# The key-value latent and the rotary key as two column halves of 288 in an encoder block

## The reference

```python
h = rms_norm(x, norm_mix_g[l])
z = h @ w_in[l]                      # columns: 4096 conv | 512 c_q | 512 c_kv | 64 k_pe | 4096 gates
u_conv, c_q, c_kv, k_pe, gate_logits = jnp.split(z, IN_SPLITS, axis=-1)
...
q = (rms_norm(c_q, q_norm_g) @ w_uq).reshape(B, S, 16, 128 + 64)
kv = (rms_norm(c_kv, kv_norm_g) @ w_ukv).reshape(B, S, 16, 128 + 128)
k_pe = apply_rope(k_pe, cos, sin)    # one rotary key for all 16 heads
```

## Time and profile before

| | us |
|---|---|
| median of 3 runs | 1625.05 (1625.01 to 1625.73) |
| the profiled execution | 1625.55 |
| its span | 1623.6 |
| query latent on TensorE, about | 190.1 to 212.8 |
| rotary key's products | 212.8 to 218.2 |
| key-value latent | 218.2 to 241.7 |
| first attention pair from | 241.7 |

### The profile page before, as it was taken

One profiled execution on the slowest core, in us unless ns is written; L12 is line 12 of the kernel. 1 busy time (PEld: TensorE's weight loads), 2 busy tenths in 40 slices (PEclk: granted clock), 3 DMA queues, 4 the chain that ended last, 5 costly groups with the idle time before them and its releaser, 6 DMA issues.

```text
span 1623.6 us, 22861 instructions
## 1 busy us (share of the span) xinstructions
PE 1613.6 (99%) x8210; PEld 1374.6 (85%) x8210; DVE 1102.3 (68%) x1486; ACT 816.8 (50%) x1040; POOL 71.0 (4%) x156
## 2 busy tenths in 40 slices
PE   9999999999999999999999999999999999999998
PEld 7888888888888888888889888888888888888886
DVE  5588889888888898665556656555555555546654
ACT  6444456555555556744446655334443454335543
POOL 6500010000000000000000000000000000000000
PEclk9999999999999999999999999999999999999999
DMA  7666655556555666667665566666666666666664
GB/s 248 202 191 184 192 156 171 175 175 182 176 163 174 215 201 193 186 190 255 186 194 147 164 184 192 195 192 185 194 193 192 189 187 196 192 189 192 187 188 145
DMA packets 161004, 304.97 MB, mean 188 GB/s; under 512 B 11657, under 2 KB 19969, under 8 KB 160513
## 3 DMA queue, kind: packets, MB, share of 16 engines
q1 hardware_dynamic: 159552, 299.41, 61.2%
q0 software_dynamic: 1056, 3.46, 0.6%
q10 hardware_dynamic: 320, 1.06, 0.2%
HBM read 301.78 MB, written 2.10 MB: 187 GB/s over the span
## 4 chain that ended last, share of the span: by engine, by line
PE 98%; ACT 1%; DVE 0%; DMA 0%; issue 0%; ACTq 0%
PE ps L1402 21%; PE ps L1404 21%; PE ps L1403 21%; PE ps L1810 15%; PE ps L1812 7%; PE ps L1415 1%; PE ps L1561 1%; PE ps L1560 1%; PE ps L1559 1%; PE ps L1614 1%; PE ps L1613 1%; PE ps L1582 0%; PE ps L1584 0%; PE ps L1707 0%; PE ps L1577 0%; PE ps L1583 0%
## 5 line engine op out<-in xcount | busy, mean ns | idle before, releaser
L923 DVE TENSOR_TENSOR wlo<-raw,whi 128x1024 fp32r<-128x1024 f32 x560 | 684.4, 1225 | 410.4 <-ACT whi L555 409.3
L555 ACT ACTIVATE whi<-raw 128x1024 fp32r<-128x1024 f32 x560 | 591.4, 1060 | 590.8 <-PE ps L1404 420.0
L1810 PE MATMUL ps<-a_both,whi 128*128 128x512 f32 x1024 | 321.9, 396 | 0.0
L1402 PE MATMUL ps<-whi,c_hi 128*128 128x512 f32 x752 | 293.5, 390 | 0.0
L1404 PE MATMUL ps<-whi,c_lo 128*128 128x512 f32 x752 | 292.9, 389 | 0.0
L1403 PE MATMUL ps<-wlo,c_hi 128*128 128x512 f32 x752 | 292.9, 389 | 0.0
L1402 PE MATMUL ps<-whi,a_both 128*128 128x512 f32 x700 | 277.4, 396 | 0.0
L1404 PE MATMUL ps<-whi,a_both 128*128 128x512 f32 x700 | 273.0, 390 | 0.0
L1403 PE MATMUL ps<-wlo,a_both 128*128 128x512 f32 x700 | 272.9, 390 | 0.0
L1812 PEld LDWEIGHTS ps<-a_both,wlo 128*128 128x128 f32 x1024 | 192.5, 188 | 45.3
L978 DVE SCALAR_TENSOR_TENSOR acc<-hconv,cwk,acc 128x256 f32<-128x256 f32 x464 | 205.2, 498 | 13.2 <-PE ps L1614 13.2
(11 more groups left out here) (272 smaller groups left out, 1342.6 us busy)
## 6 DMA issues: line engine op xcount, KB each, us to landing
raw<-in_w_ff_dram SPq DMA_DIRECT2D x256, 512.0 KB, 4.2
raw<-in_w_in_dram SPq DMA_DIRECT2D x144, 512.0 KB, 3.8
raw<-in_w_mla_out_dram SPq DMA_DIRECT2D x32, 512.0 KB, 4.2
raw<-in_w_conv_out_dram SPq DMA_DIRECT2D x32, 512.0 KB, 4.3
raw<-in_w_out_dram SPq DMA_DIRECT2D x32, 512.0 KB, 4.3
raw<-in_w_ukv_dram SPq DMA_DIRECT2D x16, 512.0 KB, 3.8
raw<-in_w_xkv_dram SPq DMA_DIRECT2D x16, 512.0 KB, 4.1
raw<-in_w_uq_dram SPq DMA_DIRECT2D x16, 384.0 KB, 3.6
```

The lines of the kernel that those rows point to most:

```text
L555: act.activation(whi[:, s, :], raw[:, s, :], ACT.Copy).then_inc(hi_ready, 1)
L923: dve.tensor_tensor(wlo[:, s, :], raw[:, s, :], whi[:, s, :].bitcast(F32), ALU.subtract).then_inc(lo_ready, 1)
L1402: pe.matmul(sum_, x_hi[:, k0 + k, tok], w_hi, start=(first and k == 0), stop=False)
L1810: pe.matmul(both, whi[:, s, cols[n]], a_both[:, :, k0 + k, :], start=(first and k == 0), stop=False)
```

## The change

The 512 latent columns and the 64 rotary columns, which lie side by side in `w_in`, are taken together as 576 and cut into two halves of 288 (`LW`). The upper half comes first: the last 224 latent columns and the 64 rotary ones. Each half takes eight units of two contraction tiles by 288 columns (576 values a partition, 288 KB), with the activations standing and 288 weight columns streaming: 192 products of 288 columns in place of 96 of 512 and 48 of 256. The upper half's sum goes to banks 0 and 1, the lower half's to banks 4 and 5.

The rotary key now comes out in token rows, so `kpe_sum`, its copy and its two transposes go; `kpe_row` is made from the sum after the eighth unit. The rotated key is turned as before, into bank 6. The row sums of the latent's squares are made in two parts: of the upper half's 224 columns in the middle of the stage (`ss_kv`, which VectorE turns into `kv_base`, 1/512 of it plus epsilon), of the lower half's 288 at the end, with one root for each 128 tokens that takes `kv_base` as its bias. The scaled rows are written by four copies. VectorE's 33 convolution steps of this stage are shared over sixteen units in place of eight. The query latent's turn stands after the fourth unit in place of the third.

```diff
--- before.py
+++ after.py
...
+LW = (LORA + ROPE) // 2
...
 UPC = KT // 2
 U_CONV = 0
 U_CQ = U_CONV + 2 * CH * UPC
-U_KPE = U_CQ + UPC
-U_CKV = U_KPE + 1
-U_ATT = U_CKV + UPC
+U_CKV = U_CQ + UPC
+U_ATT = U_CKV + 2 * UPC
 ATT_UNITS = 4 + UPC
 U_MLA = U_ATT + PAIRS * ATT_UNITS
 U_XKV = U_MLA + CH * UPC
...
-SS_KV = SS_Q + TT
+SS_KV = SS_Q + 2 * TT
...
-        kpe_sum = at(o + 20480, "kpe_sum", [ROPE, SEQ])
...
+        ss_kvb, kv_base = st(62), st(64)
...
             return ps[:, 2, 0:SEQ], ps[:, 3, 0:SEQ], ps[:, 6, 0:SEQ]
 
         block = ctx.enter_context(nc.Block())
+
+        def filled(u, r):
+
+            return 2 * LW if isinstance(r, int) and r == 0 and U_CKV <= u < U_CKV + 2 * UPC else UE
 
         def wait(eng, s, value):
 
...
                 load_chunk(U_CONV + 2 * UPC, i * (2 * UPC), w_in, i * NC + (COL_G + NC))
                 load_chunk(U_CONV + 3 * UPC, i * (2 * UPC), w_in, i * NC + (COL_A + NC))
             load_chunk(U_CQ, 0, w_in, COL_CQ)
-            load(U_KPE, 0, w_in[:, :, COL_KPE:COL_KPE + ROPE], KT, ROPE)
-            load_chunk(U_CKV, 0, w_in, COL_CKV)
+            for half in range(2):
+                col = COL_CKV + LW * (1 - half)
+                for k in range(UPC):
+                    load(U_CKV + UPC * half + k, 0, w_in[:, 2 * k:2 * k + 2, col:col + LW], 2, LW)
 
             with sp.Fori(0, PAIRS) as j:
                 r = j * ATT_UNITS
...
                 s = u % RING
                 act.wait_ge(landed[s], 16 * (u // RING + 1) + r * (16 // RING))
                 wait(act, used, u - RING + 1 + r)
-                act.activation(whi[:, s, :], raw[:, s, :], ACT.Copy).then_inc(hi_ready, 1)
+                n = filled(u, r)
+                act.activation(whi[:, s, 0:n], raw[:, s, 0:n], ACT.Copy).then_inc(hi_ready, 1)
 
             def turn_out(turn, dst, k0, gain=None, banks=(0, 1), first=6):
 
...
             square_sums(sq_lat, rows[:, 0, :, :], ss_q)
             act.wait_ge(ss_ready, SS_Q)
             root(sd_q, ss_q, LORA)
-            hi(U_KPE + LEAD)
             act.wait_ge(vec_ready, 2)
-            for k in range(UPC):
+            for k in range(2 * UPC):
                 hi(U_CKV + k + LEAD)
-                if k == 0:
-                    act.wait_ge(used, U_KPE + 1)
-                    act.activation(kpe_sum[:], ps[0:ROPE, 4, 0:SEQ], ACT.Copy).then_inc(kpe_out, 1)
-                if k == 1:
+                if k == 3:
+                    turn_out(T_CQ, cq_hi, 0, V_QG)
+                if k == UPC:
+                    act.wait_ge(used, U_CKV + UPC)
+                    for t in range(TT):
+                        last = act.activation(kpe_row[:, t, :], ps[:, t, LW - ROPE:LW], ACT.Copy, scale=rs_x[:, t:t + 1])
+                    last.then_inc(kpe_ready, 1)
+                    act.wait_ge(ss_ready, SS_Q)
+                    for t in range(TT):
+                        act.activation(sq_lat[:, t, 0:LW - ROPE], ps[:, t, 0:LW - ROPE], ACT.Square, scale=rs_x[:, t:t + 1],
+                                       accum_out=ss_kv[:, t:t + 1]).then_inc(ss_ready, 1)
+                if k == UPC + 4:
                     act.wait_ge(kpe_turned, 1)
-                    for t in range(TT):
-                        last = act.activation(kpe_row[:, t, :], ps[:, 5, ROPE * t:ROPE * (t + 1)], ACT.Copy, scale=rs_x[:, t:t + 1])
-                    last.then_inc(kpe_ready, 1)
-                if k == 2:
-                    turn_out(T_CQ, cq_hi, 0, V_QG)
-                if k == 5:
-                    act.wait_ge(kpe_turned, 2)
-                    act.activation(kpeT[:], ps[:, 5, 0:SEQ], ACT.Copy).then_inc(kpeT_ready, 1)
-            act.wait_ge(used, U_CKV + UPC)
-            act.wait_ge(ss_ready, SS_Q)
+                    act.activation(kpeT[:], ps[:, 6, 0:SEQ], ACT.Copy).then_inc(kpeT_ready, 1)
+            act.wait_ge(used, U_CKV + 2 * UPC)
             for t in range(TT):
-                act.activation(sq_lat[:, t, :], ps[:, t, :], ACT.Square, scale=rs_x[:, t:t + 1], accum_out=ss_kv[:, t:t + 1]).then_inc(ss_ready, 1)
-            act.wait_ge(ss_ready, SS_KV)
-            root(sd_kv, ss_kv, LORA)
+                act.activation(sq_lat[:, t, LW - ROPE:LORA], ps[:, 4 + t, 0:LW], ACT.Square, scale=rs_x[:, t:t + 1],
+                               accum_out=ss_kvb[:, t:t + 1]).then_inc(ss_ready, 1)
+            act.wait_ge(ckv_based, 1)
+            for t in range(TT):
+                act.wait_ge(ss_ready, SS_KV - TT + t + 1)
+                last = act.activation(sd_kv[:, t:t + 1], ss_kvb[:, t:t + 1], ACT.Sqrt, bias=kv_base[:, t:t + 1], scale=1.0 / LORA)
+            last.then_inc(sd_ready, 1)
             act.wait_ge(ckv_scale, 1)
-            scaled_rows(rows[:, 1, :, :], 0, LORA, rs_kv, chunk_out)
+            for t in range(TT):
+                act.activation(rows[:, 1, t, LW:LORA], ps[:, t, 0:LW - ROPE], ACT.Copy, scale=rs_kv[:, t:t + 1])
+                last = act.activation(rows[:, 1, t, 0:LW], ps[:, 4 + t, 0:LW], ACT.Copy, scale=rs_kv[:, t:t + 1])
+            last.then_inc(chunk_out, 1)
 
 
             def pair(j, first):
...
 
                 s = u % RING
                 dve.wait_ge(hi_ready, u + 1 + r)
-                dve.tensor_tensor(wlo[:, s, :], raw[:, s, :], whi[:, s, :].bitcast(F32), ALU.subtract).then_inc(lo_ready, 1)
+                n = filled(u, r)
+                dve.tensor_tensor(wlo[:, s, 0:n], raw[:, s, 0:n], whi[:, s, 0:n].bitcast(F32), ALU.subtract).then_inc(lo_ready, 1)
 
             def bank_blocks(b):
                 return ps[:, 6 + b, :].rearrange("p (k s) -> p k s", k=2)
...
             dve.tensor_scalar(qs, rs_q, SM, None, ALU.mult).then_inc(qs_ready, 1)
             for h in range(2):
                 dve.tensor_scalar(nqs[:, TT * h:TT * (h + 1)], rs_q, -SM, None, ALU.mult).then_inc(qs_ready, 1)
-            lo(U_KPE + LEAD)
             dve.wait_ge(vec_ready, 2)
-            for k in range(UPC):
+            for k in range(2 * UPC):
                 lo(U_CKV + k + LEAD)
-                if k == 2:
+                if k == 3:
                     turn_low(T_CQ, cq_lo, cq_hi, 0, V_QG)
-                if k == UPC - 1:
+                if k == UPC + 1:
+                    dve.wait_ge(ss_ready, SS_Q + TT)
+                    dve.tensor_scalar(kv_base, ss_kv, 1.0 / LORA, EPS, ALU.mult, ALU.add).then_inc(ckv_based, 1)
+                if k == 2 * UPC - 1:
                     reciprocal(rs_kv, sd_kv, R_KV)
                     dve.wait_ge(rs_ready, R_KV)
                     dve.tensor_tensor(rs_kv, rs_kv, rs_x, ALU.mult).then_inc(ckv_scale, 1)
-                conv_run(CONV_A, CONV_B, UPC + k, 2 * UPC)
+                conv_run(CONV_A, CONV_B, 2 * UPC + k, 4 * UPC)
 
 
             dve.wait_ge(mask_ready, 3)
...
                 if k == 2:
                     pe.wait_ge(chunk_out, N_CQ)
                     turn(T_CONV + CH - 1, rows[:, 0, :, :], 0, copied_out(T_CONV + CH - 2))
-            pe.wait_ge(conv_step, 1)
-            pe.wait_ge(lo_ready, U_KPE + 1)
-            s = U_KPE % RING
-            for k in range(KT):
-                w_hi, w_lo = (w[:, s, ROPE * k:ROPE * (k + 1)] for w in (whi, wlo))
-                pe.matmul(ps[0:ROPE, 4, 0:SEQ], w_hi, a_hi[:, k, :], start=(k == 0), stop=False)
-                pe.matmul(ps[0:ROPE, 4, 0:SEQ], w_lo, a_hi[:, k, :], start=False, stop=False)
-                mm = pe.matmul(ps[0:ROPE, 4, 0:SEQ], w_hi, a_lo[:, k, :], start=False, stop=(k == KT - 1))
-            mm.then_inc(used, 1)
             for k in range(UPC):
-                unit(U_CKV + k, 0, a_hi, a_lo, 2 * k, 0, k == 0, k == UPC - 1)
-                if k == 0:
-                    pe.wait_ge(kpe_out, 1)
-                    pe.wait_ge(vec_ready, 2)
-                    for t in range(TT):
-                        tr = pe.transpose(ps[:, 5, ROPE * t:ROPE * (t + 1)], kpe_sum[:, P * t:P * (t + 1)], ident[0:ROPE, 0:ROPE])
-                    tr.then_inc(kpe_turned, 1)
-                if k == 2:
+                unit(U_CKV + k, 0, a_hi, a_lo, 2 * k, 0, k == 0, k == UPC - 1, width=LW)
+                if k == 3:
                     pe.wait_ge(chunk_out, N_CQ + 1)
                     turn(T_CQ, rows[:, 0, :, :], 0, copied_out(T_CQ - 1))
+            pe.wait_ge(conv_step, 1)
+            pe.wait_ge(vec_ready, 2)
+            for k in range(UPC):
+                unit(U_CKV + UPC + k, 0, a_hi, a_lo, 2 * k, 4, k == 0, k == UPC - 1, width=LW)
                 if k == 4:
+                    pe.wait_ge(turn_lo, 2 * splits_before(T_CQ) + 2)
                     pe.wait_ge(kpe_rotated, 4)
                     for t in range(TT):
-                        tr = pe.transpose(ps[:, 5, P * t:P * (t + 1)], kpe_rot[:, t, :, :].rearrange("p n f -> p (n f)"), ident[:])
+                        tr = pe.transpose(ps[:, 6, P * t:P * (t + 1)], kpe_rot[:, t, :, :].rearrange("p n f -> p (n f)"), ident[:])
                     tr.then_inc(kpe_turned, 1)
             pe.wait_ge(turn_lo, 2 * splits_before(T_CQ) + 2)
```

(3 more changed lines are left out.)

## The result

| | before | after |
|---|---|---|
| median of 17 runs each, us | 1625.58 | 1628.74 |
| profiled execution, us | 1625.55 | 1628.74 |
| its span, us | 1623.6 | 1626.9 |

The ratio is 1.0022, 95% interval 1.0015 to 1.0028: 2.4 to 4.6 us slower. Forecast were 1627.0 and a range up to 1628.6, so the direction holds and the time lies 0.14 us outside the range. Half a microsecond of that is the kernel before, whose median over 17 runs is 1625.58 and not the 1625.05 of the first three. The rest is in the trace.

A forecast was written before the change was run, and what follows sets the result against it. TensorE bound the kernel (98% of the wait chain). Its 3.2 us saving was to vanish in waits, with the turn 1.75 us later and 0.15 behind it: 1625.05 + 1.9 = 1627.0 us, range 1623.2 to 1628.6.

The forecast's parts named there:

- The wait for H3: TensorE waits 1.2 us near 217.4 for the split of H3, fourth of sixteen latent units (H0 to H15).
- TensorE's own work: Latent-stage products at 0.1275 us each and one turn's break gone: 3.2 us ahead, two left after the 1.2 us wait.
- The 0.134 that the prediction set aside: Spacing in us of 288-column products if the standing operand's load added 0.0065; TensorE's gain would be 1.9 us.
- pitches below 0.145: Spacings in us of the latent stage's 288-column products that would not enter the forecast time.
- VectorE as the clock of the stage: VectorE's work from 217.8, 19.6 us plus GpSimd's price, ends last latent unit H15's low part at 237.9, 2.35 us later.
- GpSimd beside it: GpSimd's 5.0 us key rotation, now all beside VectorE work after H11's split (twelfth latent unit), adds 0.5 us.
- A2's load and the turn: First gate unit A2's load issued 238.7, split from 243.3; key-value latent's turn 247.95, 1.75 us later; TensorE idle 3.4 us.
- Behind it every engine's order is as before and TensorE is bound again, so the 1.9 us stay to the end.: Behind the key-value latent's turn and scaled rows, the delay of 1.9 us carries unchanged to the end.
- 0.15: Behind the scaled copies, the first key-value unit's split stands before ckv_hi; some 0.15 us of it no longer hidden.
- The rival "slower": GpSimd's rotation costs VectorE 2.9 us instead of 0.5, at 0.59 per us: +4.3 us, 1629.4; chance 0.10.

The follow-up runs named there:

- the widths: The kernel before, with 84 products of 256 to 512 columns into a free bank ahead of the first pair; 1637.92 us, a single run.
- three moves: Changed kernel, pair 0's gate load first, two latent units' splits ahead of the query latent's squares, key-value squares and roots ahead of the gate split; 1623.06 us, ratio 0.9985.
- light convolution: The changed kernel, with the latent stage's 33 convolution steps on 16 columns in place of 256; 1625.34 us, ratio 1.0001.
- filler: The changed kernel, with 22 products of 256 columns that nothing reads on TensorE ahead of the scaled latent's turn; 1628.25 us, ratio 1.0015.
- five copies: The kernel before, with five copies of 512 columns on ScalarE between VectorE's reciprocal and the key-value latent's scaled rows; 1627.82 us, ratio 1.0016.

## Why the prediction was right and where it failed
- **The wait for H3**, 1.2 us forecast: 1.01. Right in place and releaser. It is shorter because the three units ahead lasted longer.
- **TensorE's own work.** The term of 0.1275 us a product was too small: from 235.54 to 240.19 there are 35 distances, 0.133 us each, and 192 x 0.0055 = 1.06 us. So TensorE was 1.06 us ahead at the first query product, not 2.0 (that the two figures are alike is chance). The 0.134 that the prediction set aside was nearer, but not for its reason, the load of the standing columns, by the widths. It cost nothing in this kernel, as the forecast said of pitches below 0.145. In the version with three moves, where TensorE doesn't wait, it is 1 us that is not won (an estimate, from the same 192 products).
- **VectorE as the clock of the stage.** Shown, by the light convolution. H15's low part was forecast for 237.9 and ended at 237.94, which is luck: counted from the stage's start it ended 0.5 us later than forecast (25.6 us against 25.1).
- **GpSimd beside it**, 0.5 us forecast: mis-sized. By its rows it is 0.9 us (three pairs of steps and three low parts longer by 0.13, 0.12, 0.12, 0.12, 0.17 and 0.09, and 0.1 for `kv_base`), and without it H15 came 0.7 us and the turn 1.2 us earlier. The execution had reached the stage 0.44 us earlier than the one of before, which hid this in the trace's own times.
- **A2's load and the turn.** Issue 238.7 forecast, 238.72; split 243.3, 243.52; turn 247.95, 247.96; idle 3.4, 3.08. The chain is right, and shown by the order of two loads alone; that the times agree to 0.1 us or so is the same luck. Counted from the stage's start the turn is 2.18 us late instead of the forecast 1.75, most of it GpSimd's share, which was priced 0.4 us too low.
- **"Behind it every engine's order is as before and TensorE is bound again, so the 1.9 us stay to the end."** This step failed. The order was as before, the speed was not: I forecast an idle of 3.4 us on TensorE and priced nothing for what its clock does behind it. Neither the sum nor a rival had the clock in it. It fell to half for 3.4 us, and the first gate unit took 1.61 us longer: 2.23 + 1.61 = 3.84 at the first key-value product, and 3.74 at the end. TensorE wasn't bound at once again either: with the clock kept at full (filler, five copies) 0.56 us were still lost behind the turn, to the waits for `ckv_lo` and the probabilities, where the forecast had 0.15. The 3.74 us are 2.18 at the turn, about 1.0 for the clock and about 0.56 for those waits. The Trainium skill (TensorE: Matmul & The Clock Gate, HAM oscillation) says that waits for data between groups of matmuls bring the clock down and make the next group slow; these traces agree, with products 0.43 us apart behind idles of 2.67 and 3.08 us. It should have been a term.
- **The rival "slower"** had a like size (+4.3) and the wrong cause: GpSimd slowed VectorE by 0.9 us in its 5.0 us of work, 0.18 us per us and not 0.59.

## What to carry to other kernels
When the bound engine is made faster, walk its new waits to the end of the next stage: a unit that is split finer shifts VectorE's and ScalarE's queues and the loads behind them. Here a load's place in SP's order was worth 3.1 us, 2.2 of it wait and the rest behind the turn, as much as the whole saving that was forecast. When the forecast holds an idle of some 2.4 us or more on TensorE, add the products behind it at half clock as a term or a rival: it cost 1.6 us in the unit behind, and about 1.0 at the end. The same change becomes a gain of 2.6 us once three groups of instructions stand elsewhere in their queues.
